# One parameter array, weights laid out by chunk, and the norm's columns turned on chip, in a two-layer diffusion backbone step

## The chip, the cores and the metric

The kernel runs on one core of a Trainium2 chip. The metric is the device time of one execution in microseconds, measured over several runs. The profiled execution is one more run, recorded by the hardware profiler; its span goes from the first to the last instruction.

## The reference

The program is one inference step of two layers over 128 context tokens (`x_prompt`) and 256 latent tokens (`x_sample`), all in float32, model width 1024:

```python
for l in range(DEPTH):                                  # DEPTH = 2
    mp = modulation(c_ctx[None, :], w_mod[l], b_mod[l]) # silu(c) @ w + b, split in 6 rows of 1024
    ms = modulation(c, w_mod[l], b_mod[l])
    hp = modulate(rms_norm(xp, g_attn[l]), mp[0], mp[1])   # h * (1 + scale) + shift
    hs = modulate(rms_norm(xs, g_attn[l]), ms[0], ms[1])
    # l = 0: grouped-query attention, 16 heads, 4 kv heads, q/k normed, 2-D rotary on latents
    # l = 1: differential attention, 8 heads of 2 maps, g_sub norm of each head's output
    # latent tokens also attend to 128 cached context keys
    xp = xp + mp[2] * out_p;  xs = xs + ms[2] * out_s
    hp = modulate(rms_norm(xp, g_ffn[l]), mp[3], mp[4]); hs = ...
    xp = xp + mp[5] * grouped_moe(hp, w_router, b_router, w_gate[l], w_up[l], w_down[l]); xs = ...
y = rms_norm(x, g_final)
```

`grouped_moe` has 16 experts of hidden width 512, of which each token takes the two best of its best group. Outputs are both normed streams and the context's keys and values of both layers.

## The kernel before, in words

The 384 tokens are three tiles `t` of 128 rows (tile 0 is context). All engines are programmed by hand: each has one program in the order in which it is written, and semaphores tie them. `S(name)` makes a semaphore, and `at(name, l, n)` gives its value for the n-th event of layer l.

**Weights.** SyncE's queue loads everything large into `ring`, six slots of [128, 4096] float32 (2 MB each). A chunk is 512 columns of a matrix with 1024 rows; `chunk_src` (line 255) gives partition p the rows 8p to 8p+7, eight pieces of 2 KB each. The list `jobs` has the order: w_mod chunks 0 to 3 of layer 0, the three chunks of w_qkv_a, w_mod 4 to 11, then layer 1's w_mod 0 to 3 and w_o_a between them. `load` (line 264) waits until the slot's last reader is done. Ahead of load number 4 (qkv chunk 0) the queue also waits for `mod_ps` 1 (line 322), ahead of number 5 (qkv chunk 1) for `ld_cols` 32 (line 325). Then `experts` streams the 16 experts: gate, up and down of one expert are 6 MB in halves of 1 MB, in three sets of places (`wE`: two in the ring, one in `work`). The order of experts 3 to 15 is decided on chip by VectorE (`order_ready`), and each half waits for the matmuls that free its place. After layer 0's experts `jobs_b` loads w_qkv_b's chunks; chunk 3 and on wait for `ld_y2`, the last gather of y.

**Modulation.** `mod_slot(l, j)` (PE, line 525) multiplies silu of both conditioning vectors by chunk j: 32 matmuls into bank 7, in four groups of 32 partitions; `take_mod` (ScalarE, line 1423) copies the result to `modsb[:, j, :]`. A mod slot waits for the copy of the one before it. Rows 32g and 32g+1 of `modsb` hold the context's and the latents' values of 128 columns. `mod_store(l, part)` (GpSimd, line 363) adds `modsb` by accumulating DMA into `mod_d` in DRAM, preloaded with b_mod. Part 0 is chunks 0 to 3 (shift and scale of the attention norm), part 1 the other eight. `mod_cols` (line 370) then reads shift and scale back as columns, `colp`: feature on the partition.

**The start.** SyncE loads c_ctx, c, x, the constants `cf` (identity, rotary tables and so on), then the jobs. GpSimd loads b_mod and eleven small parameter arrays into tiles of their own. Each tile of x is squared (ScalarE, line 1405) and scaled (VectorE, line 891) to `xn`. PE runs mod slots 0 and 1, the 24 transposes of xn (line 534), and mod slots 2 and 3. GpSimd stores and reads back the columns; `cols(0)` (VectorE, line 897) makes `a1` = (1 + scale) * g; VectorE (line 905) and ScalarE (line 1432) write `hT` = a1 * turned xn + shift, and `project` (PE, line 547) starts.

**Layer 0's experts.** `mod_store(1, 0)` runs ahead of the gathers, `mod_cols(1)` after the first. `index_pair` (line 716) and `pick_one` (line 696) on PE, `gate_up` (line 761), `turn_h` (line 772) and `down` (line 785) do an expert. ScalarE stores its rows to `y_scratch` (line 1576), and at the end signals `y_stored` (line 1613); GpSimd gathers each token's two rows (line 437), and ScalarE scales them (line 1410). `hot1` and `xrow` are places in `modsb` that the experts' stage reuses.

## Time and profile before

| | |
|---|---|
| median of 3 runs | 1127.71 us (1127.23 to 1127.78) |
| profiled execution: its own time | 1125.02 us |
| profiled execution: span | 1122.9 us |
| mean granted TensorE clock | 0.934 |
| data moved by DMA | 325.89 MB, mean 290 GB/s |
| VectorE, ScalarE, GpSimd busy | 31%, 19%, 6% of the span |

The median is 2.7 us above the profiled execution's own time. In the views, PE is TensorE (PEld its weight loads), DVE VectorE, ACT ScalarE, POOL GpSimd, SP SyncE; "SPq L273" is the queue that line 273 fills. A record of a 128x512 matmul in float32 stands for one of its two passes, so a matmul counts twice. "issue" is time in which nothing is seen to be waited for.

### The profile page before, as it was taken

What the parts mean: (1) busy time and instruction counts of PE and PEld (TensorE: products, weight loads), DVE (VectorE), ACT (ScalarE), POOL (GpSimd) and SP (SyncE); (2) the same over time, 40 slices, a digit from 0 to 9 for tenths busy, and PEclk for the clock granted to TensorE, in tenths of its full rate; (3) what the DMA queues carried; (4) which work ended last, traced back from release to release, by engine and by line L of the source; (5) the groups of instructions that cost most, each with busy time, mean ns of one, the idle gap of its engine ahead of it and who ended that gap; (6) DMA issues with size and microseconds to landing.
All of it is one profiled execution on the core that took longest, in us unless ns stands there. A gap on an engine that the chain in (4) does not pass through costs nothing.

```text
span 1122.9 us, 13881 instructions
## 1 busy us (share of the span) xinstructions
PE 932.8 (83%) x5316; PEld 452.7 (40%) x5316; DVE 350.8 (31%) x872; ACT 213.9 (19%) x558; POOL 64.1 (6%) x94
## 2 busy tenths in 40 slices
PE   1599899996899898992499999788958998989940
PEld 1444678544333332330244446554433333333310
DVE  1204655246232121110502205773552411211105
ACT  2202454012000000000310005661111000000012
POOL 2100010100000000002000000001000000000020
PEclk9899999987999999997599999989969999999985
DMA  9792859429899999999822427754266999999972
GB/s 284 262 374 76 313 194 409 159 109 367 329 417 417 417 419 418 415 419 399 312 75 75 145 80 225 264 192 167 112 256 237 411 416 419 418 418 417 419 255 102
DMA packets 91715, 325.89 MB, mean 290 GB/s; under 512 B 7196, under 2 KB 7468, under 8 KB 75244
## 3 DMA queue, kind: packets, MB, share of 16 engines
q1 hardware_dynamic: 75168, 280.91, 64.2%
q0 software_dynamic: 10704, 34.40, 8.5%
q10 hardware_dynamic: 5760, 9.44, 2.3%
q8 instruction: 56, 0.92, 0.3%
q14 instruction: 27, 0.22, 0.1%
HBM read 306.27 MB, written 18.55 MB: 289 GB/s over the span
## 4 chain that ended last, share of the span: by engine, by line
PE 66%; DMA 16%; DVE 9%; SPq 3%; ACT 3%; issue 2%; POOL 1%; ACTq 0%; DVEq 0%; POOLq 0%
PE PS L547 24%; PE PS L761 17%; PE PS L785 8%; DMA ring<-in_w_up_dram 7%; DMA work<-in_w_up_dram 5%; PE PS L525 3%; PE PS L627 3%; PE PS L594 2%; PE PS L609 2%; DMA ring<-in_w_mod_dram 2%; SPq L273 1%; PE PS L696 1%; SPq L283 1%; DMA work<-y_scratch,rti 1%; PE PS L671 1%
## 5 line engine op out<-in xcount | busy, mean ns | idle before, releaser
L547 PE MATMUL PS<-ring,work 128*128 128x512 f32 x624 | 279.5, 611 | 10.2 <-ACT work L1432 10.2
L547 PEld LDWEIGHTS PS<-ring,work 128*128 128x128 f32 x624 | 122.0, 197 | 163.2 <-issue 163.2
L761 PE MATMUL PS<-ring,gate_bc 128*64 128x512 f32 x704 | 156.7, 595 | 7.5 <-DMA ring<-in_w_up_dram 3.6
L1254 DVE TENSOR_TENSOR gate_bc<-gate_bc,PS 128x256 f32<-128x256 f32 x36 | 15.1, 421 | 274.4 <-ACT gate_bc L1565 274.4
L761 PEld LDWEIGHTS PS<-ring,gate_bc 128*64 128x64 f32 x704 | 51.2, 137 | 98.5 <-issue 93.5
L785 PE MATMUL PS<-ring,work 128*64 128x512 f32 x384 | 87.2, 595 | 2.3 <-issue 2.3
L525 PE MATMUL PS<-ring,cs 128*32 128x128 f32 x1536 | 53.5, 298 | 29.9 <-DMA ring<-in_w_mod_dram 27.7
L761 PE MATMUL PS<-work,gate_bc 128*64 128x512 f32 x320 | 73.0, 607 | 1.8 <-DMA work<-in_w_up_dram 1.7
L1565 ACT ACTIVATE gate_bc<-PS 128x256 f32<-128x256 f32 x36 | 13.8, 384 | 293.1 <-PE PS L761 293.1
L525 PEld LDWEIGHTS PS<-ring,cs 128*32 128x32 f32 x1536 | 45.9, 121 | 35.6 <-DMA ring<-in_w_mod_dram 28.4
L1480 ACT ACTIVATE work<-PS,nm 128x384 f32<-128x384 f32 (+1 forms) x96 | 48.2, 511 | 5.6 <-DVE nm L983 5.3
L785 PEld LDWEIGHTS PS<-ring,work 128*64 128x64 f32 x384 | 28.2, 137 | 50.8 <-issue 50.8
L1571 ACT ACTIVATE work<-PS 128x512 f32<-128x512 f32 x36 | 21.5, 597 | 140.8 <-PE PS L785 140.8
L627 PE MATMUL PS<-work,gate_bc 128*128 128x64 f32 (+1 forms) x336 | 46.5, 279 | 0.9 <-DVE work L1022 0.5
L785 PE MATMUL PS<-work 128*64 128x512 f32 x192 | 43.6, 596 | 2.3 <-issue 1.1
L627 PEld LDWEIGHTS PS<-work,gate_bc 128*128 128x128 f32 x336 | 41.9, 194 | 4.1 <-issue 3.2
L983 DVE TENSOR_REDUCE nm<-PS 128x2 f32<-128x768 f32 (+1 forms) x48 | 37.2, 777 | 17.6 <-PE PS L594 16.8
L761 PEld LDWEIGHTS PS<-work,gate_bc 128*64 128x64 f32 x320 | 23.8, 139 | 44.2 <-issue 44.2
L609 PE MATMUL PS<-cf,work 128*128 128x128 f32 x168 | 29.7, 295 | 13.3 <-DVE work L1000 13.3
L594 PE MATMUL PS<-work 64*128 64x384 f32 (+1 forms) x192 | 37.4, 470 | 2.2 <-DVE work L971 1.4
L411 POOL DMA_INDIRECT modsb<-h_scratch,idxi x14 | 13.5, 962 | 386.1 <-DVE idxi L1243 386.1
L1259 DVE COPY work<-PS 128x256 f32<-128x256 f32 x36 | 15.3, 424 | 63.7 <-PE PS L772 63.6
(228 smaller groups left out, 809.0 us busy)
## 6 DMA issues: line engine op xcount, KB each, us to landing
ring<-in_w_mod_dram SPq DMA_DIRECT2D x24, 2048.0 KB, 13.2
ring<-in_w_gate_dram SPq DMA_DIRECT2D x44, 1024.0 KB, 21.6
ring<-in_w_up_dram SPq DMA_DIRECT2D x44, 1024.0 KB, 22.7
ring<-in_w_down_dram SPq DMA_DIRECT2D x44, 1024.0 KB, 16.9
work<-in_w_gate_dram SPq DMA_DIRECT2D x20, 1024.0 KB, 20.2
work<-in_w_up_dram SPq DMA_DIRECT2D x20, 1024.0 KB, 21.7
work<-in_w_down_dram SPq DMA_DIRECT2D x20, 1024.0 KB, 21.8
ring<-in_w_qkv_b_dram SPq DMA_DIRECT2D x6, 2048.0 KB, 24.2
```

The source lines that it names most:

```text
L525: mm = pe.matmul(PS[32 * g:32 * g + 32, 7, 0:P], cs[:, k, :], ring[:, s, 512 * k + P * g:512 * k + P * (g + 1)], start=(k == 0), stop=(k = ...
L547: mm = pe.matmul(PS[:, 2 * t, :], lhs[:, k, P * t:P * (t + 1)], ring[:, s, 512 * k:512 * (k + 1)], start=(k == 0), stop=(k == KC - 1))
L594: mm = pe.matmul(PS[:, 2 * (i % 2) + m, 0:nk], qT[64 * m:64 * m + 64, pr, P * t:P * (t + 1)], kT[64 * m:64 * m + 64, pr // 4 if l == 0 els ...
L609: tr = pe.transpose(PS[:, pT_bank(l, i, m), P * c:P * (c + 1)], pr_[:, i % 2, m, P * c:P * (c + 1)], ident)
L627: mm = pe.matmul(out, ptt[:, i % 2, m, P * c:P * (c + 1)], vals, start=(c == 0), stop=(c == len(bl) - 1))
L761: mm = pe.matmul(PS[64 * g:64 * g + 64, 4 * b + 1, :], xTx[:, k, :] if b else xTp[:, k, CAP * (e % 2):CAP * (e % 2 + 1)], w[:, 0:2, 512 * ...
L785: mm = pe.matmul(PS[64 * g:64 * g + 64, 4 * b + 3, :], hTt[:, b, f % 2, 64 * (f // 2):64 * (f // 2) + 64], w[:, 1024 * f + 512 * g:1024 * ...
L983: dve.tensor_reduce(nm[:, i % 2, :], PS[:, 2 * (i % 2):2 * (i % 2) + 2, 0:nk], X, ALU.max, negate=True).then_inc(S("nm_ready"), 1)
L1254: dve.tensor_tensor(hE[:, b, :], sg[:, b, :], PS[:, 4 * b + 1, 256:512], ALU.mult).then_inc(tile_sem(f"h_{tag(b)}", l), 1)
L1259: dve.tensor_copy(hTt[:, b], PS[:, 4 if b else 2, 0:256].rearrange("p (c n) -> p c n", c=2)).then_inc(tile_sem(f"hT_{tag(b)}", l), 1)
L1480: ins = act.activation(pr_[:, i % 2, m, 0:nk], PS[:, 2 * (i % 2) + m, 0:nk], ACT.Exp, bias=nm[:, i % 2, m:m + 1], accum_out=sm[:, i % 4, m ...
L1571: act.activation(ys[:, buf, :], PS[:, 4 * b + 3, :], ACT.Copy).then_inc(tile_sem(f"y_{tag(b)}", l), 1)
```

## The change

On the host: w_mod, w_qkv and w_o are laid out so that each chunk is one block with 16 KB in a row per partition; the two conditioning vectors are one array; g_attn, the attention norm's part of b_mod, g_q_a, g_k_a, g_sub_b, w_router and b_router are appended to the constants (`params`, 1212 columns for 764); the four lambda vectors are one array, repeated over the partitions. w_qkv's rows are dealt out as 128k + p, so `xn` is transposed in contiguous pieces.

On chip: SyncE's queue loads cond, w_mod chunk 0, x, params, and then the rest of the jobs without the two waits; the lambdas come behind chunk 3. GpSimd has no small parameter loads, and no store and reload of the columns. `turn_cols` transposes `modsb[:, 0:4, :]` on PE, and `cols` on VectorE adds the bias and picks out the columns; for layer 1 both happen inside layer 0's expert stage, in bank 3. `hot1` moves to modsb 4 to 6.

```diff
+def chunks(w):
+    d, n = w.shape[-2:]
+    w = w.reshape(w.shape[:-2] + (P, d // P, n // 512, 512))
+    return np.ascontiguousarray(np.moveaxis(w, -2, -4)).reshape(w.shape[:-4] + (n // 512, P, d // P * 512))
...
-        hot1 = modsb[:, 0:3, :]
+        hot1 = modsb[:, 4:7, :]
...
-        def chunk_src(w, j):
-            return w.rearrange("(p k) n -> p k n", k=KC)[:, :, 512 * j:512 * (j + 1)]
...
-                sp.dma_start(ring[:, s, :].rearrange("p (k n) -> p k n", k=KC), chunk_src(src, j)).then_inc(w_ready[s], 16)
+                sp.dma_start(ring[:, s, :], src[j]).then_inc(w_ready[s], 16)
...
-            sp.dma_start(cvec[:, 0, :], t_["c_ctx"].rearrange("(p k) -> p k", k=KC)).then_inc(S("ld_c"), 16)
-            sp.dma_start(cvec[:, 1, :], t_["c"][0].rearrange("(p k) -> p k", k=KC)).then_inc(S("ld_c"), 16)
-            sp.dma_start(x[:, 0, :], t_["x_prompt"][0]).then_inc(S("ld_x"), 16)
-            sp.dma_start(x[:, 1:3, :], t_["x_sample"][0].rearrange("(t p) n -> p t n", p=P)).then_inc(S("ld_x"), 16)
-            sp.dma_start(cf[:], t_["consts"]).then_inc(S("ld_const"), 16)
+            sp.dma_start(cvec[:].rearrange("p v k -> p (v k)"), t_["cond"]).then_inc(S("ld_c"), 16)
             for n, (kind, l, j, _s) in enumerate(jobs):
-                if n == 4:
-                    sp.wait_ge(S("mod_ps"), 1)
-                if n == 5:
-                    sp.wait_ge(S("ld_cols"), 32)
                 load(kind, l, j)
+                if n == 3:
+                    sp.dma_start(lamv.rearrange("p a b -> p (a b)"), t_["lam"]).then_inc(S("ld_lam"), 16)
+                if n == 0:
+                    sp.dma_start(x[:, 0, :], t_["x_prompt"][0]).then_inc(S("ld_x"), 16)
+                    sp.dma_start(x[:, 1:3, :], t_["x_sample"][0].rearrange("(t p) n -> p t n", p=P)).then_inc(S("ld_x"), 16)
+                    sp.dma_start(cf[:], t_["params"]).then_inc(S("ld_par"), 16)
...
-            def mod_cols(l):
-                pool.wait_ge(*at("mod_stored", l, 32))
...
             def gather_x(l, pair):
                 pool.wait_ge(*at("idx_ready", l, pair))
                 if pair > 1:
                     pool.wait_ge(*at("x_picked_main", l, pair - 1))
+                elif l == 0:
+                    pool.wait_ge(S("cols_turned"), 2)
...
-            mod_store(0, 0)
-            mod_cols(0)
+            pool.wait_ge(S("lam_dots"), 1)
             cache(0)
-            mod_store(0, 1)
+            mod_store(0)
...
+            def turn_cols(l, bank):
+                pe.wait_ge(*at("mod_sb", l, 4))
+                for j in range(4):
+                    tr = pe.transpose(PS[:, bank, P * j:P * (j + 1)], modsb[:, j, :], ident)
+                tr.then_inc(S("cols_turned"), 1)
...
                 def down(b, e, nth):
+                    if l == 0 and e == 0 and not b:
+                        pe.wait_ge(S("cols_ready"), 2)
...
                     if e == 0:
                         index_pair(1)
+                        if l == 0:
+                            turn_cols(1, 3)
                         pick_one(1)
...
                     mod_slot(0, 2)
                     mod_slot(0, 3)
+                    turn_cols(0, 6)
...
-            def cols(l):
-                dve.wait_ge(*at("ld_cols", l, 32))
-                dve.wait_ge(S("ld_par"), 16 * 11)
+            def cols(l, bank):
+                dve.wait_ge(*at("cols_turned", l, 1))
+                if l == 1:
+                    dve.wait_ge(S("hT_act"), NT)
+                turned = PS[:, bank, :].rearrange("p (m j g v c) -> p m j g v c", m=2, j=2, g=4, c=1)
+                for vec in range(2):
+                    ins = dve.tensor_tensor(colp[:, vec, :, :].rearrange("p m (j g) -> p m j g", j=2),
+                                            turned[:, :, :, :, vec, 0],
+                                            bcol[:, l, :, :].rearrange("p m (j g) -> p m j g", j=2), ALU.add)
+                done(ins, "cols_ready", l + 1)
                 for vec in range(2):
                     ins = dve.scalar_tensor_tensor(a1[:, vec, :], colp[:, vec, 1, :], 1.0, gcol[:, l, :], ALU.add, ALU.mult)
...
                 expert(0)
+                if l == 0:
+                    cols(1, 3)
                 expert(1)
```

SyncE's queue at the start of the program, before. The names are destination and source of a load, the bracket the semaphores it waits for:

```order
L314 DMA cvec<-in_c_ctx_dram 128x8
L315 DMA cvec<-in_c_dram 128x8
L316 DMA x<-in_x_prompt_dram 128x1024
L317 DMA x<-in_x_sample_dram 128x2x1024
L318 DMA cf<-in_consts_dram 128x764
L273 DMA ring<-in_w_mod_dram 128x8x512 x4
L273 DMA ring<-in_w_qkv_a_dram 128x8x512 [waits mod_ps]
L273 DMA ring<-in_w_qkv_a_dram 128x8x512 [waits ld_cols]
```

The same of the changed kernel:

```order
L348 DMA cvec<-in_cond_dram 128x16
L307 DMA ring<-in_w_mod_dram 128x4096
L354 DMA x<-in_x_prompt_dram 128x1024
L355 DMA x<-in_x_sample_dram 128x2x1024
L356 DMA cf<-in_params_dram 128x1212
L307 DMA ring<-in_w_mod_dram 128x4096 x3
L352 DMA gate_bc<-in_lam_dram 128x256
L307 DMA ring<-in_w_qkv_a_dram 128x4096 x2
L307 DMA ring<-in_w_qkv_a_dram 128x4096 [waits mod_ps]
```

Chunk 0 of w_mod has moved ahead of x, and the first two qkv chunks wait for nothing.

TensorE in layer 0's experts, between the first expert's gate and up (L761 before, L775 now) and the pick of the second expert's rows, before:

```order
L761 MATMUL PS<-ring,gate_bc 64x512 x7
L716 MATMUL PS<-cf,modsb 128x1 [waits one_hot_main]
L716 MATMUL PS<-cf,modsb 128x1 x2
L696 MATMUL PS<-work 64x512 x6
L772 MATMUL PS<-cf,gate_bc 128x128 [waits h_main]
```

The same of the changed kernel:

```order
L775 MATMUL PS<-ring,gate_bc 64x512 x7
L730 MATMUL PS<-cf,modsb 128x1 [waits one_hot_main]
L730 MATMUL PS<-cf,modsb 128x1 x2
L540 MATMUL PS<-cf,modsb 128x128 [waits mod_sb]
L540 MATMUL PS<-cf,modsb 128x128 x3
L710 MATMUL PS<-work 64x512 x6
L786 MATMUL PS<-cf,gate_bc 128x128 [waits h_main]
```

The four transposes of L540 stand ahead of the pick.

## Rows read from the trace of the kernel before

**Rows 1.** The page's busy times: us, share of the span, instructions

```profile
PE 932.8 (83%) x5316; PEld 452.7 (40%) x5316; DVE 350.8 (31%) x872; ACT 213.9 (19%) x558; POOL 64.1 (6%) x94
```

**Rows 2.** The chain that ended last, in order of time: start us, us, what

```profile
19.79 19.82 DMA ring<-in_w_mod_dram
39.66 2.00 PE PS L525 x64
43.16 2.57 DMA mod_scratch<-modsb
...
50.77 64.67 PE PS L547 x144
...
123.35 2.57 PE PS L580 x22
...
562.83 116.73 PE PS L547 x272
```

**Rows 3.** Windows in layer 0's experts; last three: clock, DMA share, GB/s

```profile
312.00:412.00 100.00, 96.92 (x468) 35.37 (x466) 20.45 (x62) 7.85 (x16) 3.86 (x4) 1.00 1.02 418
300.00:304.00 4.00, 4.00 (x22) 1.25 (x18) 0.86 (x3) 0.38 (x1) 0.00 (x0) 1.00 0.14 28
```

**Rows 4.** Waits of SyncE's queue, 220 to 560 us: total us, times, longest

```profile
SPq L286 <- PE PS L785: 77.7, 22, 14.1
```

**Rows 5.** Windows at the start, and one of chunk loads alone (61 to 80)

```profile
0.00:10.00 10.00, 0.00 (x0) 0.00 (x0) 0.07 (x1) 1.50 (x2) 8.00 (x19) 1.00 0.77 213
10.00:20.00 10.00, 0.00 (x0) 0.00 (x0) 3.21 (x9) 5.13 (x10) 0.00 (x0) 1.00 0.99 266
20.00:30.00 10.00, 4.74 (x88) 4.00 (x92) 0.00 (x0) 0.27 (x1) 0.00 (x0) 1.00 1.05 393
30.00:40.00 10.00, 7.53 (x148) 6.74 (x144) 0.00 (x0) 0.53 (x2) 0.00 (x0) 1.00 0.99 368
61.00:80.00 19.00, 19.00 (x45) 8.36 (x44) 0.00 (x0) 1.29 (x3) 0.00 (x0) 1.00 1.05 387
```

**Rows 6.** GpSimd's DMA queue, 0 to 45 us: packets, MB, share of 16 engines

```profile
q0 software_dynamic: 513, 0.45, 10.5%
```

**Rows 7.** Timeline: start us, us, engine line op out<-in [idle before <-releaser]

```profile
3.13 20.16 SPq L273 DMA_DIRECT2D ring<-in_w_mod_dram  x4
...
12.80 1.06 ACT L1405 ACTIVATE work<-x 128x1024 f32<-128x1024 f32 x1 [9.73 <-DMA x<-in_x_sample_dram]
...
18.63 0.75 DVE L891 TENSOR_SCALAR work<-x,rs 128x1024 f32<-128x1024 f32 x1
...
23.48 3.64 PE L525 MATMUL PS<-ring,cs 128*32 128x128 f32 x64 [23.48 <-DMA ring<-in_w_mod_dram]
...
32.34 2.96 PE L534 MATMUL PS<-cf,work 128*128 128x128 f32 x24
...
48.84 0.24 DVE L897 SCALAR_TENSOR_TENSOR a<-colp,gcol 128x8 f32<-128x8 f32 x2 [29.46 <-DMA colp<-mod_scratch]
...
279.19 0.66 PE L706 MATMUL PS<-cf,work 128*128 128x128 f32 x4 [0.69 <-ACT work L1545]
```

**Rows 8.** Timeline of both layers' y_stored signal and third scaling of y

```profile
522.64 0.19 ACT L1613 COPY ss<-cf 1x1 f32<-1x1 f32 x1 [6.22 <-DMA y_scratch<-work]
...
539.01 1.15 ACT L1410 ACTIVATE work<-work,small 128x1024 f32<-128x1024 f32 x1 [1.35 <-DMA work<-y_scratch,rti]
...
1085.99 0.19 ACT L1613 COPY ss<-cf 1x1 f32<-1x1 f32 x1 [3.16 <-DMA y_scratch<-work]
...
1099.31 1.15 ACT L1410 ACTIVATE work<-work,small 128x1024 f32<-128x1024 f32 x1 [1.40 <-DMA work<-y_scratch,rti]
```

**Rows 9.** Windows in which the granted clock (third from the end) fell

```profile
45.00:47.00 2.00, 0.00 (x0) 0.00 (x0) 0.00 (x0) 0.00 (x0) 0.99 (x2) 0.70 0.04 3
240.00:242.00 2.00, 2.00 (x13) 2.00 (x13) 0.65 (x2) 1.18 (x3) 0.00 (x0) 0.59 0.17 68
```

More of the change, by code:

```diff
@@ L36, with chunks_kp, params, cols @@
 C_RANK = C_KEY + E
-C_N = C_RANK + E
-RANK_AT = [0, 1, 2] + [3 + r for r in (9, 5, 3, 6, 0, 7, 2, 8, 1, 10, 4, 11, 12)]
+C_G = C_RANK + E
+C_B = C_G + 2 * 8
+C_QK = C_B + 2 * 2 * 8
+C_SUB = C_QK + 2 * 64
+C_LAM = C_SUB + P
+C_WR = C_LAM
+C_BR = C_WR + 8 * E
+C_N = C_BR + E
+RANK_AT = [0, 1, 2] + [3 + r for r in (9, 5, 3, 6, 0, 7, 2, 8, 1, 10, 4, 11, 12)]
+def chunks(w):
+    d, n = w.shape[-2:]
+    w = w.reshape(w.shape[:-2] + (P, d // P, n // 512, 512))
+    return np.ascontiguousarray(np.moveaxis(w, -2, -4)).reshape(w.shape[:-4] + (n // 512, P, d // P * 512))
+def chunks_kp(w):
+    d, n = w.shape[-2:]
+    w = w.reshape(w.shape[:-2] + (d // P, P, n // 512, 512))
+    return np.ascontiguousarray(np.moveaxis(np.moveaxis(w, -4, -3), -2, -4)).reshape(w.shape[:-4] + (n // 512, P, d // P * 512))
+def params(i):
+    c = shape_constants()
+    def cols(v):
+        return np.moveaxis(v.reshape(v.shape[:-1] + (8, P)), -1, 0).reshape(P, -1)
+    c[:, C_G:C_B] = cols(i["g_attn"])
+    c[:, C_B:C_QK] = cols(i["b_mod"].reshape(2, N_MOD, D)[:, 0:2])
+    c[:, C_QK:C_SUB] = np.concatenate([i["g_q_a"][0], i["g_k_a"][0]])
+    c[:, C_SUB:C_LAM] = i["g_sub_b"][0]
+    c[:, C_WR:C_BR] = i["w_router"].reshape(P, 8 * E)
+    c[:, C_BR:C_N] = i["b_router"]
+    return c
 def shape_constants():
@@ L421, in moe_dmas @@
                     gather_x(l, pair)
-                    if l == 0 and pair == 1:
-                        pool.wait_ge(*at("hT_act", 0, 3))
-                        pool.wait_ge(*at("hT_dve", 0, 3))
-                        mod_cols(1)
                 if l == 1:
@@ L533, in norm_transposes @@
                     for c in range(4):
-                        tr = pe.transpose(PS[:, g, P * c:P * (c + 1)], xn[:, t, 4 * half + c::KC], ident)
+                        tr = pe.transpose(PS[:, g, P * c:P * (c + 1)], xn[:, t, P * (4 * half + c):P * (4 * half + c + 1)], ident)
                     tr.then_inc(S("xn_turned"), 1)
@@ L1669 @@
     arrays, tensors = {}, {}
-    for name, a in [(n, np.ascontiguousarray(inputs[n])) for n in _INS] + [("consts", shape_constants())]:
+    given = {n: np.ascontiguousarray(inputs[n]) for n in _INS}
+    laid = {n: chunks(given[n]) for n in ("w_mod", "w_o_a", "w_o_b")}
+    laid |= {n: chunks_kp(given[n]) for n in ("w_qkv_a", "w_qkv_b")}
+    laid["cond"] = np.ascontiguousarray(np.concatenate([given["c_ctx"].reshape(P, KC), given["c"][0].reshape(P, KC)], 1))
+    laid["params"] = params(given)
+    laid["lam"] = np.tile(np.concatenate([given[f"lam_{n}"][0] for n in ("q1", "k1", "q2", "k2")]), (P, 1))
+    gone = ("c", "c_ctx", "g_attn", "g_q_a", "g_k_a", "g_sub_b", "lam_q1", "lam_k1", "lam_q2", "lam_k2", "w_router", "b_router")
+    for name, a in [(n, laid.get(n, given[n])) for n in _INS if n not in gone] + [(n, laid[n]) for n in ("cond", "params", "lam")]:
         arrays[f"in_{name}_dram"] = a
```

64 lines of the change are left out of this document (25 added, 39 removed).

## The prediction

> **What bounds the kernel now.** The page first: TensorE is busy 83% of the span [rows 1], but that is an average over stages with different limits. The chain that ended last tells them apart [rows 2]. Read it from the top: until 39.66 us nothing but the loads of w_mod leads to the end; then one mod slot on TensorE, two round trips of small DMAs (one to mod_scratch, one back to colp), the ScalarE half of hT, and from 50.77 the first projection. From there the chain is TensorE in layer 0's attention, then the stream of expert weights. So the chain has a first stage, 0 to 50.77 us, that is DMA and latency; this is the stage that the change edits. Everything behind it is tied to it: the weight slots of the ring come free by TensorE's progress, and even in the experts' stage, where the DMA engines move 418 GB/s for 100 us at a share of 1.02, the stream first had a hole (share 0.14 in 300 to 304 us) [rows 3], since the queue waits for slots that TensorE frees, 77.7 us in all behind the down matmuls [rows 4]. A stream that starts from TensorE's progress moves with it, so I expect a gain at the start to arrive at the end nearly whole.
>
> Inside the first stage the DMA engines are full from about 2.4 us, but at 213 and 266 GB/s for 20 us, against 393 later [rows 5]. The row of the GpSimd queue says why: 513 packets with 0.45 MB take 10.5% of 45 us, 4.7 us of all 16 engines [rows 6]. The sum of the bytes is what counts: 2.1 + 2.7 + 3.9 + 3.7 = 12.4 MB by 40 us.
>
> **The change, part by part.**
> *1. Order and bytes of the first loads.* What must land before mod slot 3 can run is, after the change, 8.39 MB of w_mod, 1.57 of x, 0.62 of params, 0.10 of b_mod, 0.01 of cond: 10.7 MB. Before it was 10.8 MB (8.39 + 1.57 + 0.39 + 0.45), and the fourth slot's matmuls started at 39.66, when about 12.3 MB had moved: a load is complete some 1.5 MB after its own last byte is due. At mod slot 0 (23.48 us [rows 7]) the same sum gives 6.2 - 4.5 = 1.7 MB, so this lag is regular; I keep 1.5 MB. The rate is open: chunks cut into 2 KB pieces move 387 GB/s, expert weights, in pieces of 4 and 8 KB, 418 [rows 3, 5]. The chunks now have 16 KB per partition, so the ends are 387 and 418 and I take 403, between, since part of the bytes (x, params) stays in 4 to 5 KB pieces. 12.2 MB / 0.403 = 30.3 us, + 2.4 us of start = **32.7 us** (31.6 to 33.9). qkv's chunk 0 comes 0.13 (lam) + 2.10 MB later: 14.4 MB, 38.1 us (36.9 to 39.6).
> *2. The waits on the queue.* Gone are mod_ps and ld_cols ahead of the first two qkv chunks. Before, chunk 1 was held until the columns landed, and that was no loss: the projection reads it 10 us after its start. Now all follow at once; cost 0, gain only by part 1.
> *3. The columns on chip.* Before: slot 3 starts 39.66, ends 41.66; a1 starts 48.84; hT 49.12; projection 50.77 [rows 2, 7]. From the slot's end to hT were 7.5 us. Now: copy of the slot 0.3, four transposes, 0.7 [rows 7], two additions and two a1 operations, all of 8 or 16 columns. The a1 pair took 0.24 [rows 7]; I give both pairs and their semaphores 0.7. Sum 1.7 us. So slot 3 32.7 to 34.7, hT at 36.4, projection's operand at 38.0; the chunk is there at 38.1. **Projection starts at 38.1 instead of 50.77: -12.7 us.** The norm of x is cover: x now stands behind a chunk. Its lag included it lands at (2.1 + 1.6 + 1.5) / 0.403 + 2.4 = 15.3, not 12.8; the squares and scalings then take 6.6 us (12.80 to 19.4 [rows 7]), slot 1 starts at about 22.5, and slot 1, 24 transposes and slot 2 (3.6 as slot 0, 3.0, 2.0 [rows 2, 7]) end at 31, 1.7 us before slot 3 lands. If that cover goes, see rival B.
> *4. Small loads of GpSimd.* Eleven are gone from its queue; their 4.7 us of engine time is already in part 1. cache(0) now waits for lam_dots (about 42 us) instead of the columns; its keys are first read at 123 [rows 2] minus the shift, 110, far later: 0.
> *5. Layer 1's columns.* mod_store(1, 0) and two loads leave GpSimd's stretch before the first gather. That is no gain: the gather waits for idx, not for them. In their place TensorE does four transposes between index_pair(1) and pick_one(1), on the path, since TensorE paces the slots there: **+0.7 us** [rows 7]. The additions on VectorE (0.7 us) come while TensorE is in a gate and up of 7 us: 0. The new waits of down(0, 0) and of the first gather are met by then: 0.
> *6. Chunks in 16 KB pieces later on.* In layer 0's attention no TensorE wait is for a chunk: 0. In the tail of layer 0's experts three qkv chunks share the engines with the store and gathers of y: from y_stored to the third scaling 16.4 us here against 13.3 us in layer 1, where no chunk is behind [rows 8]. At 387 instead of 418 GB/s three chunks cost 3 x 0.40 = 1.2 us. Ends: 0 and -3.1; I take **-1.2**, the difference of rates.
> *7. TensorE's clock.* It fell to half (1.2 GHz) in 45 to 47 us, some 4 us after slot 3, and the projection's start ran at half: its 144 records took 64.67 us, where 272 records of layer 1's took 116.73, 0.43 each, which makes 61.8 of 144 [rows 2]: 2.8 us lost. In 240 to 242 us it fell between transposes and small matmuls though TensorE was at work [rows 9]. The new gap has 3.4 us with four transposes in it. I take a fall again, so 0; the other end is -2.8. The Trainium skill ("TensorE: Matmul & The Clock Gate", Part 4: PE-mode transpose) says that transposes don't count as busy for the clock as other matmuls do; that sides with a fall, and the trace's 240 us row doesn't contradict it.
>
> **Sum: -12.7 + 0.7 - 1.2 = -13.2 us.** The profiled execution took 1125.0; with it 1111.8. The median of the runs is 2.7 higher, 1127.7, so the forecast is **1114.5**.
>
> **A rule that speaks against part of it.** The rows give 387 GB/s in 2 KB pieces and 418 in larger ones. If the difference is not the piece, mod slot 3 lands at 33.9, qkv 0 at 39.6, the projection starts there and the tail gains nothing: -11.2 + 0.7 = -10.5, 1117.2. This is rival A. The Trainium skill ("DMA: Bandwidth & Descriptors", Specifications) puts full rate at 512 bytes and more, and by it the layout would be worth nothing; the rates just named speak against it.
>
> **The rivals.**
> A. Layout without effect on rates: 1117.2. For: the 387 may come from w_mod's rows lying 24 KB apart, or from the mix; against: the two rates [rows 3, 5]. 17%.
> B. x behind a chunk: if x lands with the load behind it (20.4 instead of 15.3 us), norms, slot 1, transposes, slot 2 and slot 3 follow in TensorE's order and slot 3 ends at 38.5; projection 42.0: gain 8.8 + 0.5 = 9.3, 1118.4. For: before, x shared the engines with the small loads; against: it landed first. 10%.
> C. The clock doesn't fall, because the gap is short: 1114.5 - 2.8 = 1111.7. For: it did not fall in the gap between slots 2 and 3 (granted 1.00 in 30 to 40 us [rows 5]); against: the row at 240 [rows 9]. 25%.
> D. Slower. Nothing holds the queue now, and up to five chunks are issued behind slot 3's. If loads in flight share the engines, slot 3 is complete only with the three qkv chunks and the next mod chunk: 10.7 + 0.1 + 6.3 + 2.1 = 19.2 MB, 50.0 us; + 5.3 = 55.3, +4.5; with +0.7 and -1.2: 1131.7. It decides from a projection later than 51.3. For: before, issuing the four mod chunks took 20.16 us [rows 7], so only some were ever in flight, and 16 KB pieces let more in. Against: they landed in order, (39.66 - 23.48) / 3 = 5.4 us apart. 4%.
> E. The expert stream sets the end whatever starts before it: only the tail's -1.2 stays, 1126.5. Against: the hole in 300 to 304. 3%.
>
> **How the numbers follow.** My case 41%, A 17, B 10, C 25, D 4, E 3. A measurement of this kernel tells about 0.2% (2.3 us) from nothing. Faster: all but D and E, 93%, less 1 for what I don't see: 0.92; same 0.03; slower 0.05. My case with its ends (rate, lag of 1 to 1.7 MB, tail 0 to -3.1) is 1111 to 1117; C at its best end is 1109, B at its worst 1120. Range 1109 to 1120.
>
> **What would show it.** Projection's first matmul near 38; mod slots on TensorE at about 12, 22, 29 and 33; about 1.7 us from slot 3's end to hT; the clock's row in 34 to 45; 400 GB/s or more from 5 to 30 us; TensorE 0.7 us later in the first expert, relative to pick_one(0); y_stored to third scaling of layer 0 below 16.4. Wrong if the shift at the projection is not still there at the first expert or after the last: then the wait is elsewhere.

## The result, and the profile after

| | before | after |
|---|---|---|
| median, runs side by side on one chip (4 each) | 1127.6 us | 1109.76 us (1107.19 to 1114.24) |
| ratio after / before, 95% interval | | 0.9846 [0.981, 0.9883] |
| profiled execution: its own time, span | 1125.02, 1122.9 | 1107.7, 1105.5 |
| mean granted TensorE clock | 0.934 | 0.935 |

The change gains 17.8 us, 1.5%; the forecast was 1114.5, its range 1109 to 1120. The kernel before, run beside the experiments below, spread from 1119.8 to 1130.0 us over 44 executions. Single times therefore say little about differences under 3 us, and most of what follows is read from places inside the traces.

The page of the changed kernel: its span, the engines, the packets and the granted clock in 40 slices.

```profile
span 1105.5 us, 13880 instructions
...
PE 927.1 (84%) x5324; PEld 451.4 (41%) x5324; DVE 351.2 (32%) x876; ACT 214.0 (19%) x558; POOL 51.5 (5%) x75
...
PEclk8999999978999999995799999899959999999985
...
DMA packets 57764, 325.84 MB, mean 295 GB/s; under 512 B 6541, under 2 KB 6797, under 8 KB 36557
```

The bytes are the same as before to within 0.1 MB. The chain that ended last, answering to [rows 2] (start, us, what):

```profile
5.33 30.71 DMA ring<-in_w_qkv_a_dram
36.16 62.05 PE PS L561 x144
...
498.38 11.15 DMA y_scratch<-work
...
545.90 116.73 PE PS L561 x272
```

The first stage is now loads alone: both round trips of small DMAs are gone from the chain, and the projection starts at 36.16 us, where it was 50.77. Further down a new row stands out: the last stores of y take 11.15 us of the path. The windows of the start (us, PE, PEld, DVE, ACT, POOL busy, granted clock, DMA share, GB/s), for [rows 5]:

```profile
0.00:10.00 10.00, 0.00 (x0) 0.00 (x0) 0.07 (x1) 1.50 (x2) 2.14 (x8) 1.00 0.77 289
10.00:20.00 10.00, 3.36 (x64) 2.83 (x64) 2.29 (x7) 4.95 (x10) 0.00 (x0) 0.87 1.04 438
20.00:30.00 10.00, 8.11 (x152) 7.25 (x152) 0.92 (x2) 0.86 (x4) 0.00 (x0) 0.79 1.00 419
30.00:40.00 10.00, 6.45 (x77) 3.92 (x78) 5.43 (x21) 5.74 (x14) 0.12 (x1) 1.00 1.02 433
```

Before, these moved 213, 266, 393 and 368 GB/s. The GpSimd queue's row over the first 45 us was 10.5% of the 16 engines [rows 6] and is now:

```profile
q0 software_dynamic: 96, 0.22, 1.3%
```

The timeline of the start (start, busy, then in brackets the idle time ahead and its releaser), for [rows 7]:

```profile
10.95 3.36 PE L532 MATMUL PS<-ring,cs 128*32 128x128 f32 x64 [10.95 <-DMA ring<-in_w_mod_dram]
14.58 1.06 ACT L1434 ACTIVATE work<-x 128x1024 f32<-128x1024 f32 x1 [11.83 <-DMA x<-in_x_sample_dram]
21.00 3.46 PE L532 MATMUL PS<-ring,cs 128*32 128x128 f32 x64 [6.68 <-DMA ring<-in_w_mod_dram]
24.38 2.84 PE L548 MATMUL PS<-cf,work 128*128 128x128 f32 x24
30.84 1.95 PE L532 MATMUL PS<-ring,cs 128*32 128x128 f32 x64 [1.73 <-DMA ring<-in_w_mod_dram]
33.18 0.65 PE L540 MATMUL PS<-cf,modsb 128*128 128x128 f32 x4 [0.39 <-ACT modsb L1452]
34.23 0.24 DVE L923 SCALAR_TENSOR_TENSOR a<-colp,cf 128x8 f32<-128x8 f32 x2
34.51 4.30 ACT L1461 ACTIVATE work<-PS,colp,a 128x128 f32<-128x128 f32 x12 [1.38 <-DVE a L923]
```

From the last mod slot's end (30.84 + 1.95 = 32.79) to hT (34.51) are 1.7 us, where 7.5 were. The same shape of timeline at the end of layer 0's experts, for [rows 8]:

```profile
487.92 3.65 PE L775 MATMUL PS<-ring,gate_bc 128*64 128x512 f32 x16 [1.14 <-DMA ring<-in_w_up_dram]
497.25 0.60 ACT L1600 ACTIVATE work<-PS 128x512 f32<-128x512 f32 x1 [5.26 <-PE PS L801]
509.71 0.19 ACT L1642 COPY ss<-cf 1x1 f32<-1x1 f32 x1 [11.86 <-DMA y_scratch<-work]
523.40 1.15 ACT L1439 ACTIVATE work<-work,small 128x1024 f32<-128x1024 f32 x1 [1.59 <-DMA work<-y_scratch,rti]
```

Putting both traces side by side at the same instructions tells where the time went:

| place | before | after | shift |
|---|---|---|---|
| layer 0's projection starts | 50.77 | 36.16 | -14.6 |
| its 144 records end | 115.44 | 98.21 | -17.2 |
| attention's last product starts | 199.79 | 182.56 | -17.2 |
| first expert's gate and up start | 280.54 | 261.19 | -19.35 |
| second expert's | 293.90 | 275.04 | -18.9 |
| last gate and up | 506.49 | 487.92 | -18.6 |
| y_stored | 522.64 | 509.71 | -12.9 |
| third scaling of y | 539.01 | 523.40 | -15.6 |
| layer 1's 272 projection records start | 562.83 | 545.90 | -16.9 |
| end of the span | 1122.9 | 1105.5 | -17.4 |

The shift made in the first 36 us is still there at the end, as the prediction argued. On the way it grows: by 2.6 us in the projection's records, by 2.1 between attention and the first expert, and by 1.8 behind the third scaling. The tail of layer 0's experts, from the last gate and up to the third scaling of y, takes 3.0 us of it back.

### The profile page after: what moved, and what is told of

It reads as the page before. It is cut to its first block, busy times and chain, and to the rows that moved or that the text cites. A ratio compares the mean times of both kernels' runs of the same rounds, so it can differ in the third digit from the quotient of the medians.

```text
span 1105.5 us, 13880 instructions
## 1 busy us (share of the span) xinstructions
PE 927.1 (84%) x5324; PEld 451.4 (41%) x5324; DVE 351.2 (32%) x876; ACT 214.0 (19%) x558; POOL 51.5 (5%) x75
## 4 chain that ended last, share of the span: by engine, by line
PE 62%; DMA 20%; DVE 9%; ACT 3%; issue 2%; SPq 2%; POOL 1%; ACTq 0%; DVEq 0%; POOLq 0%
PE PS L561 24%; PE PS L775 14%; DMA work<-in_w_up_dram 7%; PE PS L801 7%; DMA ring<-in_w_up_dram 7%; PE PS L532 3%; PE PS L641 3%; DMA ring<-in_w_qkv_a_dram 3%; PE PS L608 2%; PE PS L623 2%; SPq L317 2%; PE PS L710 1%; DMA y_scratch<-work 1%; DMA work<-y_scratch,rti 1%; DVE nm L1009 1%
## 5 line engine op out<-in xcount | busy, mean ns | idle before, releaser
L561 PE MATMUL PS<-ring,work 128*128 128x512 f32 x624 | 272.6, 598 | 3.4 <-DMA ring<-in_w_qkv_a_dram 2.3
L561 PEld LDWEIGHTS PS<-ring,work 128*128 128x128 f32 x624 | 119.2, 192 | 151.9 <-issue 149.4
L775 PE MATMUL PS<-ring,gate_bc 128*64 128x512 f32 x704 | 156.3, 595 | 5.3 <-DVE gate_bc L1294 2.5
L775 PEld LDWEIGHTS PS<-ring,gate_bc 128*64 128x64 f32 x704 | 52.1, 137 | 94.9 <-issue 89.7
L775 PE MATMUL PS<-work,gate_bc 128*64 128x512 f32 x320 | 73.0, 607 | 3.8 <-DMA work<-in_w_up_dram 3.8
L775 PEld LDWEIGHTS PS<-work,gate_bc 128*64 128x64 f32 x320 | 24.1, 139 | 45.7 <-issue 45.6
L623 PE MATMUL PS<-cf,work 128*128 128x128 f32 x168 | 29.4, 293 | 13.3 <-DVE work L1026 13.3
L548 PE MATMUL PS<-cf,work 128*128 128x128 f32 x48 | 7.8, 324 | 34.2 <-DVE work L910 34.2
## 6 DMA issues: line engine op xcount, KB each, us to landing
ring<-in_w_down_dram SPq DMA_DIRECT2D x44, 1024.0 KB, 17.2
```

The lines of the kernel that those rows point to most:

```text
L561: mm = pe.matmul(PS[:, 2 * t, :], lhs[:, k, P * t:P * (t + 1)], ring[:, s, 512 * k:512 * (k + 1)], start=(k == 0), stop=(k == KC - 1))
L623: tr = pe.transpose(PS[:, pT_bank(l, i, m), P * c:P * (c + 1)], pr_[:, i % 2, m, P * c:P * (c + 1)], ident)
L775: mm = pe.matmul(PS[64 * g:64 * g + 64, 4 * b + 1, :], xTx[:, k, :] if b else xTp[:, k, CAP * (e % 2):CAP * (e % 2 + 1)], w[:, 0:2, 512 * ...
```

## The experiments

Two things had to be settled. **At the start:** which of packing, layout, missing waits, order and on-chip columns gives the 14.6 us, and whether they add up. **In the tail:** whether the 16 KB pieces of w_qkv_b's chunks hold up the small DMAs of y, against the rival that the clock or the moved start does it. Each ratio is against the kernel before on the same chip, with its 95% interval; "slower" and "faster" mean that the interval leaves 1 out. Some cuts leave out the host's side of an edit.

### e1: before, without its two waits on the queue

```diff
-                if n == 4:
-                    sp.wait_ge(S("mod_ps"), 1)
-                if n == 5:
-                    sp.wait_ge(S("ld_cols"), 32)
```

> The kernel before without the two waits of SyncE's queue (ahead of qkv chunks 0 and 1); all else as before. Theory: the waits cost nothing, since the projection needs chunk 1 only 10 us after its start; they kept the queue clear for the column round trip, so that without them the two small round trips run beside full engines and the projection starts at 51 to 56 instead of 50.8: 0 to +5 us. Rival: the waits held the kernel back and their removal alone is worth several us: projection below 49, time below 1125.

Measured: 1133.81 us, ratio 1.0062 [1.0041, 1.0083], slower. Rows of its chain:

```profile
44.42 6.22 DMA mod_scratch<-modsb
51.70 5.33 DMA colp<-mod_scratch
58.98 64.10 PE PS L541 x144
```

The projection starts 8.2 us later than before, outside what was expected. With the engines at a share of 1.06 from 40 to 60 us, the way from the last mod slot to hT took 14.5 us instead of 7.5. The median rose by 6.9 us, also more than the 0 to 5 expected. The waits were not idle caution: they kept the engines clear for the round trip. The prediction's sentence that holding chunk 1 "was no loss" was true, but too weak; the two waits together were a gain of about 7 us.

### e2: before, with chunks in 16 KB pieces

```diff
-                sp.dma_start(ring[:, s, :].rearrange("p (k n) -> p k n", k=KC), chunk_src(src, j)).then_inc(w_ready[s], 16)
+                sp.dma_start(ring[:, s, :], src[j]).then_inc(w_ready[s], 16)
```

> The kernel before with w_mod, w_qkv and w_o laid out so that a chunk is 16 KB in a row per partition; nothing else. Theory: chunks alone move at 410 to 420 GB/s instead of 387, mod slot 3 starts about 1 us sooner than 39.66, and in the tail of layer 0's experts the last stores of y wait behind three chunks in 16 KB pieces (from the end of the last down to y_stored 12 us instead of 6.8, then gathers 3 us shorter): net -1 + 3 = about +2 us, unless the clock changes. Rival A (layout without effect on rates): 387 GB/s as before and 0 us. Third: only the gain, -2 us.

Measured: 1125.82 us, ratio 0.9987 [0.9969, 1.0004]: no difference that this measurement can tell, where +2 us was expected. The projection starts at 49.76, 1.0 us earlier. The tail shows why it is not more; y_stored in its timeline:

```profile
525.61 0.19 ACT L1618 COPY ss<-cf 1x1 f32<-1x1 f32 x1 [11.99 <-DMA y_scratch<-work]
```

The wait was 6.22 us before. Nothing else of the change is in this kernel, so the layout alone nearly doubles it.

### e3: before, with the small parameters packed

```diff
+        gqk = cf[:, C_QK:C_SUB].rearrange("p (w d) -> p w d", w=2)
+        gsub = cf[:, C_SUB:C_LAM]
...
+            sp.dma_start(lamv.rearrange("p a b -> p (a b)"), t_["lam"]).then_inc(S("ld_lam"), 16)
...
-            for l in range(2):
-                pool.dma_start(gcol[:, l, :], t_["g_attn"][l].rearrange("(p k) -> p k", k=KC)).then_inc(S("ld_par"), 16)
-            pool.dma_start(gqk[:, 0, :], bc(t_["g_q_a"][0])).then_inc(S("ld_par"), 16)
...
```

> The kernel before with the small parameters appended to the constants and the lambdas one load on SyncE's queue; the eleven loads of GpSimd are gone; layout, order of the loads, waits and column round trip as before. Theory: the 4.7 us of all 16 engines that the small packets took are gained, less 0.4 MB of larger ones (1 us): mod slot 3 starts at 36 instead of 39.66, projection near 47, time -3.5 to -4. Rival: the start is bound by latency and TensorE, not by engine time: less than 1.5 us gained.

Measured: 1120.0 us, ratio 0.9938 [0.9921, 0.9956]. Its second window:

```profile
10.00:20.00 10.00, 2.41 (x48) 2.23 (x52) 3.21 (x9) 5.12 (x10) 0.00 (x0) 1.00 1.05 391
```

391 GB/s where 266 were, with chunks in the same 2 KB pieces: the first 20 us were slow by the small loads. Mod slot 3 comes 5.9 us earlier (33.80), the projection 4.2 (46.60), because slot 3's own matmuls took 3.6 instead of 2.0 us, with a granted clock of 0.61 in 34 to 38 us; the round trip stayed. Both gains are larger than expected (slot 3 at 36, projection near 47). The median fell by 6.9 us, the span of the profiled execution by 5.3, of which 1.5 come only behind the start of layer 1's 272 records.

### e5: the change, with the columns through DRAM as before

```diff
-            pool.wait_ge(S("lam_dots"), 1)
+            mod_store(0, 0)
+            mod_cols(0)
...
-                for j in range(4):
-                    tr = pe.transpose(PS[:, bank, P * j:P * (j + 1)], modsb[:, j, :], ident)
```

> All of the change but the columns on chip: packed parameters, chunk layout, chunk 0 ahead of x, no queue waits, but shift and scale still stored to DRAM and read back as columns by GpSimd. Theory: mod slot 3 starts near 31 as in the changed kernel, then the two round trips, now beside full engines in 16 KB pieces, take 10 us or more where they took 7.2: hT at 43 or later, projection 44 to 50, so that the on-chip columns are worth 8 to 14 us of the changed kernel's start; time 1115 to 1125. Rival: the round trip keeps its 7.5 us: projection at 42, time near 1115.

The columns of both layers go through DRAM again. Besides, the two conditioning vectors are two loads and xn is transposed in strided pieces, as before the change.

Measured: 1129.13 us, ratio 1.0027 [1.0007, 1.0047]: slower than before, if by little, with packing, layout, order and no waits in it. That is outside what was expected, and so is the projection. Its chain:

```profile
5.06 26.25 DMA ring<-in_w_mod_dram
34.89 9.67 DMA mod_scratch<-modsb
45.62 6.49 DMA colp<-mod_scratch
54.05 64.84 PE PS L558 x144
```

Slot 3 ran from 31.35 to 33.31, hT only from 52.41: 19.1 us for the round trip, with nothing to hold the chunks back and the engines full. All that the loads had gained was spent on waiting for two small DMAs.

### e6: the change, with 2 KB pieces

```diff
-                sp.dma_start(ring[:, s, :], src[j]).then_inc(w_ready[s], 16)
+                if kind in ('mod', 'qkv', 'wo'):
+                    rows = "(k p) n -> p k n" if kind == "qkv" else "(p k) n -> p k n"
+                    sp.dma_start(ring[:, s, :].rearrange("p (k n) -> p k n", k=KC),
+                                 src.rearrange(rows, k=KC)[:, :, 512 * j:512 * (j + 1)]).then_inc(w_ready[s], 16)
```

> The changed kernel with the matrices left in their old layout in DRAM, so that every chunk is again 8 pieces of 2 KB per partition; all else as changed. Theory: the start is slower by the difference of rates (387 against 420 GB/s over 12.2 MB, 2.5 us: projection near 38.7 instead of 36.2), and the tail of layer 0's experts is back at 6 to 7 us from the last down's copy to y_stored with gathers of 16.4 us, 3 us better than the changed kernel: within 1 us of the changed kernel, 1108 to 1112. Rival: the layout is what makes the gain, without it 1115 or more.

Measured: 1113.67 us, ratio 0.9898 [0.9867, 0.9929]. Its window at 20 us, then y_stored in its timeline:

```profile
20.00:30.00 10.00, 5.36 (x85) 4.98 (x86) 3.06 (x8) 3.15 (x10) 0.00 (x0) 0.66 1.05 387
```

```profile
511.15 0.19 ACT L1647 COPY ss<-cf 1x1 f32<-1x1 f32 x1 [6.12 <-DMA y_scratch<-work]
```

387 GB/s against 419 in the same window of the changed kernel: the layout sets the rate, which ends rival A. The prediction had given the 24 KB between w_mod's rows as another reason for 387; w_qkv_a's rows are 6 KB apart, and the windows from 34 to 46 us, in which its chunks are loaded, show 384 to 388 GB/s too. So it is the piece, as far as these two matrices tell. The projection starts at 41.20, later than the expected 38.7, so the layout is worth 5.0 us at the start with the rest of the change in place. The rate is not all of it: when slot 3 started, at 35.45, 12.4 MB had moved, 1.7 MB above the 10.7 MB that it needs, against 11.9 MB at 30.84 in the changed kernel. The wait for the last stores is back at 6.12 us. The median is above the expected 1108 to 1112.

### e7: the change, with w_qkv_b alone in 2 KB pieces

```diff
+                if kind == "qkv" and l == 1:
+                    sp.dma_start(ring[:, s, :].rearrange("p (k n) -> p k n", k=KC),
+                                 src.rearrange("(k p) n -> p k n", k=KC)[:, :, 512 * j:512 * (j + 1)]).then_inc(w_ready[s], 16)
+                else:
+                    sp.dma_start(ring[:, s, :], src[j]).then_inc(w_ready[s], 16)
```

> The changed kernel with w_qkv_b alone in its old layout (2 KB pieces); w_mod, w_qkv_a and w_o stay in 16 KB pieces. Theory: the start is that of the changed kernel, projection near 36, and the wait for the last stores of y falls from 11.9 to about 6.2 us while the gathers take 16.4 instead of 13.7: 2.5 to 3 us faster than the changed kernel, 1105 to 1108. Rival: the long wait has another cause than the size of the pieces (its place in time, more loads in flight): it stays at 12 us, 0 us.

Measured: 1108.52 us, ratio 0.9851 [0.9824, 0.9877]. The wait is 6.10 us, the start untouched (projection at 35.81). Only the chunks behind the experts differ, so it is they that hold up y. The total was expected at 1105 to 1108 and can't be told from the changed kernel's. It says little: between the projection's start and the last gate and up this execution took 4.1 us longer than the changed kernel's (455.9 against 451.8), none of which the edit touches.

### e8: the change, with all of w_qkv_b behind the gathers

```diff
-                if (kind, j) == ("qkv", 3):
+                if (kind, j) == ("qkv", 0):
                     sp.wait_ge(S("ld_y2"), 32)
```

> The changed kernel with SyncE's wait for the last gather of y (ld_y2) moved from ahead of w_qkv_b's chunk 3 to ahead of its chunk 0, so that no chunk is in flight beside the stores and gathers of y. Theory: these then take what they take in layer 1, 3.2 us and 13.3 us, instead of 11.9 and 13.7; chunk 0 lands some 7 us after the last gather, and the projection needs it only 13 us after: 8 to 9 us faster than the changed kernel, 1099 to 1103. Rival: layer 1's projection then waits for its chunks (each 5 us of loading, two more loads of the cache beside them), and gives 4 us or more of it back.

Measured: 1101.24 us, ratio 0.9771 [0.9739, 0.9803], the lowest median here, though e13 and e10 lie within its interval. Its timeline:

```profile
506.20 0.19 ACT L1642 COPY ss<-cf 1x1 f32<-1x1 f32 x1 [3.16 <-DMA y_scratch<-work]
...
519.70 1.15 ACT L1439 ACTIVATE work<-work,small 128x1024 f32<-128x1024 f32 x1 [1.38 <-DMA work<-y_scratch,rti]
...
532.63 10.01 PE L561 MATMUL PS<-ring,work 128*128 128x512 f32 x16 [1.09 <-ACT work L1461]
```

With no chunk in flight the stores land in 3.16 us. Layer 1's projection still waits for hT (ScalarE), not for a chunk: from the third scaling to that projection 12.9 us, as in the changed kernel (536.32 - 523.40). The first transposes do wait for the chunk, until 527.23, but the second tile's wait for VectorE and set the pace. The first 16 records then took 10.01 us against 8.71 in the changed kernel; but in the kernel before they took 10.02, so that no cost of the later loads shows.

### e13: the change, with one chunk ahead of the hold

```diff
-                if (kind, j) == ("qkv", 3):
+                if (kind, j) == ("qkv", 1):
```

> The changed kernel with one w_qkv_b chunk ahead of the wait for the last gather of y (three in the changed kernel, none in the held one). Theory: the stores of y wait for what lies ahead of them in the engines, 5 us for each 2 MB chunk less the 4 us until they are issued: from the last down's copy to y_stored 3.2 us as with none, or up to 6; 7 to 9 us faster than the changed kernel, 1100 to 1104. Rival: it is not the bytes ahead but any chunk in large pieces: 10 us or more, as with three.

Measured: 1102.47 us, ratio 0.9793 [0.9764, 0.9822].

The row of y_stored in its timeline:

```profile
501.89 0.19 ACT L1642 COPY ss<-cf 1x1 f32<-1x1 f32 x1 [3.67 <-DMA y_scratch<-work]
```

Zero, one and three chunks ahead give waits of 3.16, 3.67 and 11.86 us: the price is for what is still in flight when the stores are issued (here the DMA share was 0.82 in 498 to 500 us and 0.35 in 500 to 502), not for having a chunk ahead at all.

### e9: the change, with the waits put back

```diff
+                if n == 4:
+                    sp.wait_ge(S("mod_ps"), 1)
+                if n == 5:
+                    sp.wait_ge(S("cols_turned"), 1)
```

> The changed kernel with the two waits of SyncE's queue put back: qkv chunk 0 behind mod slot 0, qkv chunk 1 behind the turned columns (the nearest thing to the old ld_cols). Theory: with the columns on chip the waits neither protect nor cost anything: chunk 0 is issued at 14 us, long before it can move, chunk 1 at 34 lands at 41 and is read at 46: within 1 us of the changed kernel. Rival: removing them was part of the gain: 3 us or more slower than the changed kernel.

Measured: 1109.41 us, ratio 0.9867 [0.9838, 0.9895], projection at 35.84. Once no round trip is left, the waits neither help nor hurt.

### e11: the change, with x and params first

```diff
+            sp.dma_start(x[:, 0, :], t_["x_prompt"][0]).then_inc(S("ld_x"), 16)
+            sp.dma_start(x[:, 1:3, :], t_["x_sample"][0].rearrange("(t p) n -> p t n", p=P)).then_inc(S("ld_x"), 16)
+            sp.dma_start(cf[:], t_["params"]).then_inc(S("ld_par"), 16)
             for n, (kind, l, j, _s) in enumerate(jobs):
```

> The changed kernel with x and the parameters ahead of w_mod's chunk 0 again. Theory: the same bytes must land before mod slot 3, so it starts at 30 to 31 as in the changed kernel and the projection at 36: within 1 us of the changed kernel. Rival: chunk 0 ahead lets TensorE run mod slot 0 early and the order is worth 2 us or more; the other way round, x behind chunk 0 made the norm late (slot 1 at 21.0 waits for it) and x first is 1 to 3 us faster.

Measured: 1110.56 us, ratio 0.986 [0.9832, 0.9887]. x's first square is at 9.04 instead of 14.58, mod slot 0 at 15.45 instead of 10.95, slot 3 at 30.16 and the projection at 35.48 against 36.16. What comes first moves the early steps and hardly the last one, which needs all the bytes.

### e12: before, with packing and on-chip columns alone

It is made from the changed kernel: pieces of 2 KB, x first and both waits are put back (the second on `cols_turned`). What is left of the change is e3's packing, the change on `cols`, `turn_cols` and `mod_store`, the one array of the conditioning vectors and the dealing of w_qkv's rows.

> Packed parameters and columns on chip, with the old layout of the matrices (2 KB pieces), x and the parameters ahead of chunk 0, and the two queue waits (chunk 1 behind the turned columns). Theory: the small loads are worth 4 to 7 us and the on-chip columns another 5.5 to 6 us (7.2 us of round trips and their issue against 1.7): projection at 40 to 41, tail as before the change, time 1113 to 1116, so that these two parts make three quarters of the whole gain. Rival: order and layout are needed for it: 1118 or more.

Measured: 1112.85 us, ratio 0.9879 [0.9851, 0.9906]; projection at 39.05, wait for the last stores 6.12 us. Packing and columns alone bring 14.2 us, four fifths of the change's gain. This kernel starts slot 3 at 32.35, 3.1 us ahead of e6, and the projection 2.1 us ahead; e6 differs in order and waits alone. At slot 3's start 11.5 MB had moved here and 12.4 in e6. So in 2 KB pieces one of these still matters, and loads in flight behind slot 3's chunk, as in rival D, are a likely reason; which one it is wasn't tried.

### e10: held chunks, and matmuls that keep TensorE busy

```diff
+            def keep_busy(n):
+                for _ in range(n):
+                    pe.matmul(PS[:, 7, 0:256], ident, cf[:, 0:256], start=True, stop=True)
...
+                            if u == 0:
+                                pe.wait_ge(S("y_scaled"), NT)
+                            if u < 2:
+                                keep_busy((6, 2)[u])
...
+                    keep_busy(5)
```

> The kernel with all w_qkv_b chunks held, and TensorE given filler matmuls (128x256 into bank 7, results unused) where it waits: five between the turned columns and layer 0's projection, six and two ahead of and between layer 1's first transposes. Theory: TensorE's granted clock is at 2.4 GHz when both projections start; layer 0's takes 61.9 us instead of 63.75, layer 1's first 16 records 7 instead of 10 us: 4 to 5 us faster than the held kernel (1101.2), 1096 to 1098. Rival: the clock does not stay up for so few, or the fillers delay the transposes as much as they save: no difference or slower.

Measured: 1102.64 us, ratio 0.9783 [0.9759, 0.9807], no gain over e8. The windows from 34 us (columns as above), first of e8, then of this kernel, and last this kernel's timeline at layer 1:

```profile
34.00:38.00 4.00, 2.21 (x4) 1.15 (x5) 3.96 (x15) 3.87 (x12) 0.00 (x0) 0.84 0.98 414
38.00:42.00 4.00, 4.00 (x8) 1.58 (x7) 2.98 (x21) 1.92 (x4) 1.12 (x2) 0.73 1.02 434
```

```profile
34.00:38.00 4.00, 3.84 (x16) 2.54 (x15) 3.67 (x14) 3.17 (x10) 0.00 (x0) 1.00 1.00 422
```

```profile
527.00 4.89 PE L546 MATMUL PS<-cf 128*128 128x256 f32 x12 [25.53 <-DMA ring<-in_w_qkv_b_dram]
...
535.57 7.11 PE L566 MATMUL PS<-ring,work 128*128 128x512 f32 x16 [1.07 <-ACT work L1471]
```

The forecast of 1096 to 1098 was missed. In layer 0 the projection's 144 records take 62.05 us instead of e8's 63.75, but so they do in two kernels without fillers (the changed one and e13), so that this isn't shown to be the fillers' doing. At layer 1 the first 16 records take 7.11 us, where all kernels without fillers took 8.5 or more. But it is a flawed experiment there. The program's wait for the first chunk stands ahead of the fillers, so they start when that chunk is there (527.00) and push the first transposes back; the projection begins 2.9 us later than e8's and has gained that back when the 272 records start (543.55 against 543.51). From the third scaling of y, which this execution reached 0.5 us earlier, the fillers even lose 0.5 us. Fillers that don't stand in the way of the transposes are left open.

## Why the prediction was right, and where it was not

**The mechanism, and that the shift reaches the end: right.** -14.6 us at the projection, -17.4 at the end. Rival B (x late behind a chunk) is out by x's first square at 14.58, and by e11, where x first gives nothing. Rival E (the expert stream sets the end) is out by the table of shifts, rival D (loads in flight share the engines and slot 3 comes late) by slots at 10.95, 21.00 and 30.84, and its price by the ratio. But D's neighbour is real: what suffers under full engines is not the next large load but a small DMA that someone waits for (e1, e5, and the tail).

**Step 1, order and bytes: right in its working, rate and lag a little off.** Slot 3 came at 30.84 instead of 32.7, outside the 31.6 to 33.9. I took 403 GB/s between 387 and 418, and 1.5 MB of lag. From 2.4 us to slot 3 the rate was 414 (399 in 5 to 10 us, where x moves, then 438 and 419), and 11.9 MB had moved by then, a lag of 1.2 MB. Each is worth about 0.8 us. The ends of the rate's range were rows of 2 KB pieces and of 4 to 8 KB pieces, and a row of 16 KB pieces did not exist; for the chunks themselves the upper end was only a lower bound. e6 has the other side: 387 GB/s and a projection 5.0 us later. By the Trainium skill's rule ("DMA: Bandwidth & Descriptors", Specifications) that full rate is reached from 512 bytes on, pieces of 2 and of 16 KB would be alike; the measurement decides, and here they are not.

**Step 2, waits removed: 0, right for the sum and wrong as a reason.** They are worth nothing only because step 3 took the round trip away (e9: 35.84 with them). Without step 3 they are worth 7 us (e1).

**Step 3, columns on chip: right to a tenth.** 1.7 us forecast, 1.7 measured from slot to hT. Yet 5.8 us, the difference to 7.5, is its price in the quiet of the kernel before. Beside the rest of the change the round trip would take 19.1 us (e5), and removing it moves the projection by 17.9 us (54.05 to 36.16). A sum of parts taken from the kernel before hides this: the parts are not independent. Packing alone gives 4.2 at the projection, layout alone 1.0, no waits alone -8.2, and all of these without the columns -3.3.

**Step 4, small loads: right.** e3's window shows 391 GB/s where 266 were, and slot 3 there comes 5.9 us earlier, more than the 4.7 us of engine time.

**Step 5, the turn in the experts: 0.5 instead of 0.7,** from the shifts at the first and second expert's gate and up.

**Step 6, the tail: wrong in sign, the step that failed.** The forecast was -1.2 with ends 0 and -3.1; measured, +3.0. I had looked at the rate of three chunks and at the gathers. From y_stored to the third scaling it did get shorter, 13.7 us against 16.4, which is 2.7 better and near my far end. What I left out is the wait ahead of them, for the last rows of y to be stored: 11.86 us instead of 6.22. The time from the last gate and up to the third scaling, which holds both:

| kernel | w_qkv_b | wait for the stores | whole tail |
|---|---|---|---|
| before | 2 KB, three ahead (so in all rows of 2 KB) | 6.22 | 32.5 |
| e6 | 2 KB | 6.12 | 32.7 |
| e7 | 2 KB | 6.10 | 32.6 |
| e12 | 2 KB | 6.12 | 32.6 |
| e1 | 2 KB | 6.09 | 32.5 |
| e3 | 2 KB | 6.10 | 32.6 |
| after | 16 KB, three ahead | 11.86 | 35.5 |
| e2 | 16 KB, three ahead | 11.99 | 35.3 |
| e9 | 16 KB, three ahead | 12.09 | 35.7 |
| e11 | 16 KB, three ahead | 11.98 | 35.2 |
| e5 | 16 KB, three ahead | 11.99 | 35.6 |
| e13 | 16 KB, one ahead | 3.67 | 27.0 |
| e8 | 16 KB, none ahead | 3.16 | 26.6 |
| e10 | 16 KB, none ahead | 3.16 | 27.0 |

This is shown, not argued: the rows fall into groups by the layout of w_qkv_b and the number of its chunks ahead, whatever else the kernel has. The windows, two of the changed kernel and one of the kernel before (columns as above), add what happens meanwhile:

```profile
504.00:508.00 4.00, 0.00 (x0) 0.00 (x0) 0.00 (x0) 0.00 (x0) 0.00 (x0) 0.50 0.97 409
508.00:512.00 4.00, 0.00 (x0) 0.00 (x0) 0.00 (x0) 0.19 (x1) 1.01 (x2) 0.50 0.33 136
```

```profile
526.00:530.00 4.00, 0.00 (x0) 0.00 (x0) 0.00 (x0) 0.00 (x0) 2.89 (x4) 0.50 1.04 395
```

In 16 KB pieces the last stores (signalled at 509.71) land when the chunks ahead are nearly all in (the windows of e2, e9 and e11 show the same), and the gathers then run on free engines; that is why they are as short as in e8 (13.5 us). In 2 KB pieces the stores land at 522.64 amid full engines, and the gathers run beside the chunks. So the two terms are one: step 6 counted the shorter gathers and not the wait that bought them. Why the stores come so late is not shown. That a DMA engine takes turns between queues piece by piece, so that each small store waits for pieces eight times as long, is how I read it; that in the large pieces the stores simply wait until what is ahead has drained fits this stage as well. e5 speaks for the turns: its small DMAs of the columns landed after 9.67 and 6.49 us with the engines at a share of 1.02 throughout. No row here shows single pieces. The Trainium skill ("DMA: Bandwidth & Descriptors", Queues, rings and completion order) tells of engines that alternate between queues by packets; e5's rows agree in kind. The bound on an unknown cost had only looked down to a gain and to zero. The 6.22 us that the store waited behind 2 KB pieces, against 3.16 in layer 1 [rows 8], was a sign that this wait, too, depends on the chunks; it could have opened the range above zero.

**Step 7, the clock: the other end came.** Rival C had 25%. The granted clock stayed at 1.00 from 30 to 40 us, and the 144 records took 62.05 us instead of 64.67, 2.6 us. It is not a sure effect of the change: of seven executions whose projection starts between 35.4 and 36.5 us, three took 62.05 (the changed kernel, e13, and e10 with its fillers) and four 63.5 to 63.75 (e7, e8, e9, e11). That the short gap makes the fall shorter is not shown: e2, which keeps the long gap of before, took 63.56 us. With a long gap no execution was without a fall (63.56 to 64.84 in before, e1, e2, e3 and e5), with the short one three of nine were without (e6 and e12 took 63.59 and 63.75), one of them with fillers. Another 2.1 us were gained between attention and the first expert, where 16 records of the output projection took 6.96 us instead of 9.39 (from 224.28, before from 242.43); and 1.3 between the third scaling and layer 1's 272 records. Nothing of the change touches these; that it is where the falls of the clock happen to lie in this execution is argued from the spans of the records, and not tested.

**How the numbers met.** Against the forecast of -13.2 for the profiled execution, -17.4: start -1.9, clock at the projection -2.6, clock before the experts -2.1, turn and experts together 0, tail +4.2, layer 1 -1.8. The median came 4.7 under the forecast, inside the range, with an error of 4.2 in the tail that errors the other way outweighed. That it stayed inside is in part luck: with the tail at the forecast -1.2 it would have been near 1105.6, below the range.

## What to carry to other kernels

Before taking away a wait that seems idle, or enlarging the pieces of a bulk load, look for a small DMA that something waits for at that time: its latency was 3.2 us alone, and with three chunks of 2 MB issued ahead 6 us in 2 KB pieces and 12 in 16 KB pieces; with one such chunk ahead, mostly in by then, it was 3.7. Hold bulk loads that have slack behind such a DMA (here 8.5 us between the medians for one number changed, 8.9 in the tail), and where a short round trip through DRAM can be replaced by work on chip, count its price with the engines full, not as the old trace shows it. When a cost is bounded by nearby rows, ask of each edit which waits besides the obvious one share its resource, and let the range reach past zero on their account.
